# Query blocks of the mixing stage in another order: in pairs from the middle outwards, four heads of each in turn

## The chip, the cores and the metric

The kernel runs as one program on one core of a Trainium2 chip. The metric is the device time of one execution in microseconds (us). Before the change three runs gave 4028.39, 4029.53 and 4033.28 us, median 4029.53 us. Engines are named as in the profile: PE is TensorE, DVE is VectorE, ACT is ScalarE, POOL is GpSimd, SP is SyncE, whose queue here issues most loads.

## What is computed

One layer of a decoder trunk with two branches, for a prompt of 2048 positions and for 32 sample rows (8 requests of 4 positions). The change touches the stage that mixes positions of the prompt. Cut to what matters there:

```python
# branch A, mLSTM, over the chunks of the prompt, in order (a running state)
s   = einsum('bhtd,bhsd->bhts', qb, kb) * dmat
num = einsum('bhts,bhsv->bhtv', s, vb) + w_inter[..., None] * einsum('bhvd,bhtd->bhtv', C, qb)
h   = num / jnp.maximum(jnp.abs(den), jnp.exp(-m_t))[..., None]
C_new = w_prev[..., None, None] * C + einsum('bhs,bhsv,bhsd->bhvd', w_s, vb, kb)
h = h * lax.rsqrt(jnp.mean(h * h, axis=-1, keepdims=True) + EPS)

# branch B, attention of 8 heads on 2 groups of keys, for each block of 128 queries:
_, sel = lax.top_k(indexer_scores(iqb, iwb, ik, visible), topk)   # 256 keys for each query
s = einsum('btngd,btknd->btngk', q, k_sel) * (B_HD ** -0.5)
p = jax.nn.softmax(where(valid, s, -inf), axis=-1)
o = einsum('btngk,btknd->btngd', p, v_sel)
```

The kernel doesn't gather the chosen keys in the prompt: it scores a block against all keys up to its own and adds a stored mask of 0 or a large negative number. Block i (0 to 15) therefore has i + 1 tiles of 128 keys, and its work grows with i. Query blocks don't depend on each other; the chunks of branch A do.

## The kernel before, in words

The mixing stage (`prompt_mixing_phase`) runs from about 2208 to 3055 us of the span. All engines walk through one list of events, written by `mixing_events`, each taking from an event what concerns it, in order. The list goes over `heads`: n = 8 i + hd, block by block and head by head. One step n of the list holds, in this order:

- N of head n + 1 (DVE: reciprocal of the sum, L1962, and scaling of the probabilities, L1964);
- the first two T of head n (PE turns four tiles of 128 x 128 into one of two banks `pg`, L1690; ACT copies the bank to `probT`, L1820). A head has one T for four key tiles, so one or two for blocks 0 to 7, three or four for blocks 8 to 15;
- one event of branch A's next chunk, by hd: M1, M2 (twice), M3 (twice), M4 (twice), Y. These are PE matmuls (L1783, L1787, L1702) with DVE and ACT work between them: M1 needs on ACT `copy_k` (L1830) and the decay matrix (L1881) and on DVE the product `sd` (L2020), before its half of `slot` is free;
- at some n an event of the 32 sample rows (K, C, W, Z, V, U, from n = 12 to 114);
- the first S of head n + 3 (`scored[:1]`), then the T of head n that are left (`turned[2:]`), then the second S (`scored[1:]`). S is a piece of up to 1024 score columns: PE L1681, then DVE L1949, which adds the mask and takes the maximum. Blocks 0 to 7 have one piece, blocks 8 to 15 two;
- E of head n + 2 (ACT: exp, L1845);
- at hd 5 the event Q: ACT takes the row norms of branch A's chunk, four squares (L1907) and a square root (L1911) for which another function table is loaded;
- after heads 3 and 7 the event O: PE multiplies the turned probabilities of four heads with the values (L1720), ACT copies the result (L1855), POOL stores it (L1531).

Results of S, M1 to M4 and L pass through two halves of `slot` in turn; T and M1 through two banks of `pg` in turn. ACT and DVE do their part of the events strictly in the list's order: a copy for head n's third T stands behind whatever the list has for ACT before it. `prob` has three buffers, one for each head that is under way.

The SP queue loads queries and mask of a block (`load_a`) and the inputs of a chunk of branch A (`load_m`), two blocks ahead, and keys and values once (`load_resident`): `FIRST_KEYS` blocks of them first, the rest behind the loads of block 1.

Of the kernel before, what the change touches and what calls it, by code (L numbers as in the profile page):

```python
# [1351 lines left out]
FIRST_SAMPLE_STEP = 12  # L1352
FIRST_KEYS = 4

# [17 lines left out]
def mixing_events():  # L1372
# [5 lines left out]

    heads = [(i, hd) for i in range(NB) for hd in range(BH)]
    sample = sample_events()  # L1380
# [36 lines left out]
def prompt_mixing_phase(nc, c, d, first, load_first, inputs, load_inputs, load_memory, early):  # L1417
# [5 lines left out]
    with ExitStack() as ctx:  # L1423
# [104 lines left out]
        def store_oT(eng, i, kv):  # L1528

            n = 2 * i + kv  # L1530
            eng.dma_start(d["ybt"][4 * kv:4 * kv + 4, :, i * P:(i + 1) * P].rearrange("t p q -> p t q"),  # L1531
                          oT[n % 2][:, :, :]).then_inc(last_stored if n == 2 * NB - 1 else oT_stored[n % 2], 16)
# [4 lines left out]
        def _(sp):  # L1537
# [55 lines left out]
            sp.wait_ge(oT_ready, 2 * NB)  # L1593
            store_oT(sp, NB - 1, 1)

        @block.gpsimd
        def _(pool):
# [38 lines left out]
            for e in events:  # L1636
# [7 lines left out]
                elif e[0] == "Y":  # L1644
                    rows = slice(i * P, (i + 1) * P)
                    pool.wait_ge(ya_ready, 4 * (i + 1))
                    pool.dma_start(d["y"][rows, 0:D].rearrange("q (h e) -> q h e", h=AH), ya[:, :, :]).then_inc(ya_stored, 16)
                elif e[0] == "O" and 2 * i + e[2] + 1 < 2 * NB:
                    pool.wait_ge(oT_ready, 2 * i + e[2] + 1)
                    store_oT(pool, i, e[2])  # L1650
# [5 lines left out]
        def _(pe):  # L1656
# [15 lines left out]
            def score_piece(e):  # L1672
                _, i, hd, q = e
                p = i % 2
                if hd == 0 and q == 0:
                    pe.wait_ge(a_loaded[p], 32 * (i // 2 + 1))
                    pe.wait_ge(k_resident[i >= FIRST_KEYS], 16)
# [6 lines left out]
            def turn_group(e):  # L1684
                _, i, hd, q = e
                if q == 0:
                    pe.wait_ge(normed, BH * i + hd + 1)
                s = take_bank(e)
                for t in range(4 * q, min(4 * q + 4, i + 1)):
                    ins = turn(pg[:, s, (t % 4) * P:(t % 4 + 1) * P], prob[(BH * i + hd) % AHEAD][:, t * P:(t + 1) * P], c["ident"][:, :])  # L1690
                ins.then_inc(turned, 1)
# [12 lines left out]
            for e in events:  # L1704
# [5 lines left out]
                elif kind == "O":  # L1710
# [6 lines left out]
                    if 2 * i + kv:  # L1717
                        pe.wait_ge(oT_ready, 2 * i + kv)
                    for t in range(i + 1):
# [92 lines left out]
        def copy_group(act, e):  # L1812
# [3 lines left out]
            act.wait_ge(turned, n + 1)  # L1816
            if hd % 4 == 0 and 2 * i + hd // 4:
                act.wait_ge(o_mm, 2 * i + hd // 4)
            t0, t1 = 4 * q, min(4 * q + 4, i + 1)
# [14 lines left out]
        def _(act):  # L1834
# [3 lines left out]
            for e in events:  # L1838
                kind, i, p = e[0], e[1], e[1] % 2
                if kind == "E":  # L1840
                    hd = e[2]
                    act.wait_ge(nbias_ready, BH * i + hd + 1)
                    if i:
                        act.wait_ge(inverse, BH * (i - 1) + hd + 1)
                    nc.scalar.activation(prob[(BH * i + hd) % AHEAD][:, 0:(i + 1) * P], prob[(BH * i + hd) % AHEAD][:, 0:(i + 1) * P], ACT.Exp,  # L1845
                                         scale=SCALE, bias=mx[:, (BH * i + hd) % AHEAD, 1:2], accum_out=sums[:, hd:hd + 1]).then_inc(p_ready, 1)
                elif kind == "T":
                    copy_group(act, e)
                elif kind == "O":
                    kv = e[2]  # L1850
                    act.wait_ge(o_mm, 2 * i + kv + 1)
                    n = 2 * i + kv
                    if n >= 2:
# [60 lines left out]
        def _(dve):  # L1914
# [20 lines left out]
            for e in events:  # L1935
                kind, i, p = e[0], e[1], e[1] % 2
                if kind == "S":
                    hd = e[2]
                    q, b = e[3], (BH * i + hd) % AHEAD
                    lo, width = pieces((i + 1) * P)[q]  # L1940
                    s = slot_filled(dve, e)
                    if q:
                        after_slot(dve, ("S", i, hd, q - 1))
                    else:
                        dve.wait_ge(a_loaded[p], 32 * (i // 2 + 1))
                    if BH * i + hd >= AHEAD:
                        j, hp = divmod(BH * i + hd - AHEAD, BH)
                        dve.wait_ge(turned, bank_no[("T", j, hp, min(2 * q + 1, key_groups(j) - 1))] + 1)
                    nc.vector.tensor_tensor_reduce(out=prob[b][:, lo:lo + width], in0=slot[:, s, 0:width],  # L1949
                                                   in1=mk[p][:, lo:lo + width], scale=1.0,  # L1950
                                                   scalar=mx[:, b, 0:1] if q else TAKEN, op0=ALU.add, op1=ALU.max,
                                                   accum_out=mx[:, b, 0:1]).then_inc(slot_free[s], 1)
                    if q + 1 == key_pieces(i):
                        after_slot(dve, e)
                        if BH * i + hd >= AHEAD:
                            dve.wait_ge(p_ready, BH * i + hd - AHEAD + 1)
                        nc.vector.tensor_scalar(mx[:, b, 1:2], mx[:, b, 0:1], -SCALE, None, ALU.mult).then_inc(nbias_ready, 1)
                elif kind == "N":
                    n = BH * i + e[2]
                    b = n % AHEAD  # L1960
                    dve.wait_ge(p_ready, n + 1)
                    nc.vector.reciprocal(rsum[:, e[2]:e[2] + 1], sums[:, e[2]:e[2] + 1]).then_inc(inverse, 1)  # L1962
                    dve.wait_ge(inverse, n + 1)
                    nc.vector.tensor_scalar(prob[b][:, 0:(i + 1) * P], prob[b][:, 0:(i + 1) * P], rsum[:, e[2]:e[2] + 1], None,  # L1964
                                            ALU.mult).then_inc(normed, 1)
# [1905 lines left out]
```

## Time and profile before

| | us |
|---|---|
| median of 3 runs (lowest, highest) | 4029.53 (4028.39, 4033.28) |
| the profiled execution's own time | 4027.08 |
| its span | 4025.5 |
| PE busy in the span | 3879.9 (96%) |
| DVE busy | 2919.6 (73%) |
| ACT busy | 1414.2 (35%) |
| POOL busy | 1661.6 (41%) |
| first and last PE start in the mixing stage | 2222.12, 3053.3 |

The profiled execution took 4027.08 us, and its span is 4025.5 us: 1.6 us lie outside the span. Its mean granted TensorE clock is 0.985 of full speed. A busy share is an average over stages that have different limits; the mixing stage is a fifth of the span, from slice 23 to slice 31 of the page's 40.

### The profile page before, as it was taken

Reading aid. Unit: us, or ns where it says so; the run is one execution under the profiler, and the core shown is the slowest. Engines: PE = TensorE matmul, PEld = TensorE weight load, DVE = VectorE, ACT = ScalarE, POOL = GpSimd, SP = SyncE. Lnnn points to the kernel's source line nnn. Section 1 sums busy time; section 2 is a strip of 40 time slices with the busy share of each in tenths; the row PEclk is TensorE's granted clock in tenths of the full one; section 3 lists DMA queues with packets and bytes.
Section 4 is the critical chain, followed back from the end, with each engine's and each line's share of the span. In section 5 each row is a group of like instructions: output and inputs, shape, how many; then the busy total and the mean of one; then the engine's idle time right before and its main releaser. Section 6 shows DMA issues by size and latency. Waiting matters only on the chain. (4 is left out here: it accounts for less than half of the span.)

```text
span 4025.5 us, 41935 instructions
## 1 busy us (share of the span) xinstructions
PE 3879.9 (96%) x14574; PEld 2324.4 (58%) x14574; DVE 2919.6 (73%) x3887; ACT 1414.2 (35%) x2616; POOL 1661.6 (41%) x1513
## 2 busy tenths in 40 slices
PE   8899999999999999999999699999998899999999
PEld 4555555564456566666665466555553788854444
DVE  4589989779999999999996566555454577653333
ACT  4411211156234423433431566555553322111111
POOL 0000035449687556666664232122103666552111
PEclk9999999999999999999999899999999999999999
DMA  5312222330111121121211643222132755531111
GB/s 220 91 53 67 65 82 85 117 121 36 60 60 64 53 71 64 63 70 63 69 61 60 186 119 105 66 90 78 61 101 79 228 166 169 173 127 68 39 53 46
DMA packets 290825, 367.35 MB, mean 91 GB/s; under 512 B 72223, under 2 KB 219443, under 8 KB 287926
## 3 DMA queue, kind: packets, MB, share of 16 engines
q1 hardware_dynamic: 250890, 249.79, 20.3%
q0 software_dynamic: 18608, 85.26, 5.7%
q10 hardware_dynamic: 21120, 29.66, 2.4%
q8 instruction: 115, 1.88, 0.2%
q14 instruction: 92, 0.75, 0.1%
HBM read 235.11 MB, written 128.23 MB: 90 GB/s over the span
## 5 line engine op out<-in xcount | busy, mean ns | idle before, releaser
L1306 DVE MAX8 best<-score 128x8 f32<-128x384 f32 (+13 forms) x448 | 639.7, 1428 | 26.5 <-POOL score L1274 11.6
L1308 DVE MATCH_REPLACE8 score<-best,score 128x384 f32<-128x384 f32 (+13 forms) x448 | 631.2, 1409 | 0.0
L1063 PE MATMUL pr<-xnT,w_row 128*128 128x347 f32 (+1 forms) x960 | 298.5, 458 | 0.0
L389 PE MATMUL pg<-xnT,wt 128*128 128x416 f32 x800 | 282.4, 516 | 0.0
L1215 POOL TENSOR_TENSOR kT<-kT 128x347 f32<-128x347 f32 (+1 forms) x240 | 193.7, 807 | 212.0 <-ACT kT L1133 204.8
L1681 PE MATMUL mix_slot<-mix_kT,mix_bq 128*128 128x512 f32 (+3 forms) x640 | 271.0, 539 | 10.3 <-DVE mix_mx L1949 4.3
L1720 PE MATMUL mix_po<-mix_probT,mix_v 128*128 128x512 f32 x544 | 240.8, 596 | 5.2 <-ACT mix_probT L1820 4.3
L1063 PEld LDWEIGHTS pr<-xnT,w_row 128*128 128x128 f32 x960 | 180.7, 190 | 106.5 <-issue 10.4
L1133 ACT COPY kT<-pr 128x347 f32<-128x347 f32 (+1 forms) x240 | 106.5, 445 | 351.9 <-PE pr L1063 341.8
L389 PEld LDWEIGHTS pg<-xnT,wt 128*128 128x128 f32 x800 | 153.1, 192 | 127.7 <-issue 127.6
L1215 POOL TENSOR_TENSOR kT<-kT,sm 128x347 f32<-128x347 f32 (+1 forms) x179 | 159.8, 893 | 125.4 <-ACT sm L1133 122.8
L1063 PE MATMUL pr<-t_room,w_row 128*128 128x347 f32 (+1 forms) x640 | 203.1, 460 | 0.0
L1093 ACT ACTIVATE relu<-relu,iws 128x512 f32<-128x512 f32 (+3 forms) x304 | 186.7, 661 | 5.0
L1820 ACT COPY mix_probT<-mix_pg 128x512 f32<-128x512 f32 (+3 forms) x320 | 153.8, 524 | 86.1 <-PE mix_pg L1690 85.6
L1133 ACT COPY sm<-pr 128x347 f32<-128x347 f32 (+1 forms) x180 | 80.2, 445 | 287.3 <-PE pr L1063 237.8
L1720 PEld LDWEIGHTS mix_po<-mix_probT,mix_v 128*128 128x128 f32 x544 | 102.1, 191 | 129.9 <-issue 128.7
L1531 POOL DMA_DIRECT2D ybt_scr<-mix_oT x31 | 24.4, 787 | 369.2 <-ACT mix_oT L1855 349.2
L1088 ACT ACTIVATE relu<-pi 128x1024 f32<-128x1024 f32 (+3 forms) x152 | 139.7, 919 | 98.4 <-POOL score L1270 47.4
L1063 PEld LDWEIGHTS pr<-t_room,w_row 128*128 128x128 f32 x640 | 121.9, 192 | 70.1 <-issue 7.0
L1681 PEld LDWEIGHTS mix_slot<-mix_kT,mix_bq 128*128 128x128 f32 x640 | 111.2, 192 | 88.5 <-issue 70.8
L995 PE MATMUL pi<-ikT,iq 64*128 64x512 f32 (+3 forms) x608 | 139.9, 577 | 12.6 <-ACT relu L1088 8.8
L1063 PE MATMUL pr<-t_room,w0b 128*128 128x347 f32 (+1 forms) x480 | 150.4, 455 | 0.0
(637 smaller groups left out, 8086.4 us busy)
## 6 DMA issues: line engine op xcount, KB each, us to landing
gt_scr<-kT SPq DMA_DIRECT2D x40, 694.0 KB, 3.3
out_gm<-gt_scr ACTq DMA_DIRECT2D x32, 520.0 KB
gt_scr<-kT SPq DMA_DIRECT2D x20, 692.0 KB, 4.2
wt<-in_w_in SPq DMA_DIRECT2D x22, 512.0 KB, 4.0
w0a<-in_w_in SPq DMA_DIRECT2D x11, 1024.0 KB, 6.7
w_row<-in_w_in SPq DMA_DIRECT2D x10, 1024.0 KB, 6.7
qt_scr<-kT POOLq DMA_DIRECT2D x8, 1040.0 KB, 4.2
early<-ybt_scr SPq DMA_DIRECT2D x4, 2080.0 KB, 10.7
```

What stands on the lines that cost most here:

```text
L389: ins = nc.tensor.matmul(pg[0:m, g, 0:GW], w[:, k, 0:m], c["xnT"][:, k, g * GW:(g + 1) * GW], start=k == 0, stop=k == KT - 1)
L995: ins = nc.tensor.matmul(pi[:, piece % 2, e, 0:width], iq[t % 2][half, h2, :], c["ikT"][half, lo:lo + width], start=True, stop=True)
L1063: ins = nc.tensor.matmul(pr[:, b, 0:w], lhs, rhs, start=k == 0, stop=k == 3)
L1088: nc.scalar.activation(relu[piece % 2][:, :, 0:width], pi[:, piece % 2, :, 0:width], ACT.Relu, scale=float(ID) ** -0.5).then_inc(relu_step, 1)
L1093: nc.scalar.activation(rl, rl, ACT.Copy, scale=iws[:, blocks[t], 2 * h2 + e:2 * h2 + e + 1]).then_inc(relu_ready, 1)
L1133: nc.scalar.copy(dst, pr[:, b, 0:GATE_WIDTHS[n % GATE_PASSES]]).then_inc(row_out, 1)
L1215: nc.gpsimd.tensor_tensor(o[:, slot, :], o[:, slot, :], term, ALU.add).then_inc(added, 1)
L1306: nc.vector.max(best[:, :], sc).then_inc(top_step, 1)
L1308: nc.vector.match_replace(sc, best[:, :], sc, TAKEN).then_inc(top_step, 1)
L1681: ins = mm(slot[:, s, a:a + m], bq[p][:, hd, :], kT[:, hd // 4, lo + a:lo + a + m], start=True, stop=True)
L1720: ins = mm(po[:, :], v[:, t, kv * HD:(kv + 1) * HD], probT[:, t, :, :], start=t == 0, stop=t == i)
L1820: nc.scalar.copy(probT[:, t0:t1, hd % 4, :], pg[:, n % 2, 0:(t1 - t0) * P].rearrange("p (t q) -> p t q", q=P)).then_inc(bank_free[n % 2], 1)
```

## The change

The list of heads no longer goes through blocks 0 to 15. Blocks are taken in pairs from the middle outwards, (7, 8), (6, 9), (5, 10), ... (0, 15), and within a pair four heads of the smaller block, four of the larger, the other four of the smaller, the other four of the larger. A group of four heads is still one O. Branch A's chunks keep their order, one chunk for eight steps of the list, now by the place n in the list instead of by block and head. All counts that engines wait for go by the place in the list (`HEAD_AT`, `GROUP_AT`, `BLOCK_AT`). `FIRST_KEYS` becomes 8, since the first block of the list is block 7. No instruction of the mathematics is added or removed.

```diff
-FIRST_KEYS = 4
+FIRST_KEYS = 8
+BLOCK_ORDER = [b for n in range(NB // 2) for b in (NB // 2 - 1 - n, NB // 2 + n)]
+GROUP_ORDER = [(b, kv) for n in range(NB // 2) for kv in range(KV) for b in BLOCK_ORDER[2 * n:2 * n + 2]]
+HEAD_ORDER = [(b, BH // KV * kv + x) for b, kv in GROUP_ORDER for x in range(BH // KV)]
+BLOCK_AT = {b: n for n, b in enumerate(BLOCK_ORDER)}
+GROUP_AT = {g: n for n, g in enumerate(GROUP_ORDER)}
+HEAD_AT = {h: n for n, h in enumerate(HEAD_ORDER)}
...
-    heads = [(i, hd) for i in range(NB) for hd in range(BH)]
+    heads = HEAD_ORDER
...
-        if i + 1 < NB:
-            m, *x = memory[hd]
-            events.append((m, i + 1, *x))
-        elif hd in (1, 2):
-            events.append(("L", hd - 1))
+        step, at = n // BH + 1, n % BH
+        if step < NB:
+            m, *x = memory[at]
+            events.append((m, step, *x))
+        elif at in (1, 2):
+            events.append(("L", at - 1))
...
-        if hd == 5 and i + 1 < NB:
-            events.append(("Q", i + 1))
+        if at == 5 and step < NB:
+            events.append(("Q", step))
...
-            def load_a(i):
-                p, rows = i % 2, slice(i * P, (i + 1) * P)
-                if i >= 2:
-                    after_slot(sp, ("S", i - 2, BH - 1, key_pieces(i - 2) - 1))
+            def load_a(n):
+                i, p = BLOCK_ORDER[n], n % 2
+                rows = slice(i * P, (i + 1) * P)
+                if n >= 2:
+                    earlier = BLOCK_ORDER[n - 2]
+                    after_slot(sp, ("S", earlier, BH - 1, key_pieces(earlier) - 1))
```

Three places show what moves. In these rows `mix_slot<-mix_kT,mix_bq` is an S, `mix_pg<-ident,...` a T (one matmul for a tile), `mix_slot<-sm_C` and the like branch A, `mix_pb<-out_w` a sample event, `mix_po` an O.

First PE, in the second half of block 13: before the change, from the last T of head 5 to the O of the block's heads 4 to 7:

```order
L1690 MATMUL mix_pg<-ident,early 128x128 x6
L1681 MATMUL mix_slot<-mix_kT,mix_bq 128x512
L1681 MATMUL mix_slot<-mix_kT,mix_bq 128x384
L1690 MATMUL mix_pg<-ident,mix_prob 128x128 x8
L1702 MATMUL mix_slot<-sm_C 128x257 x2
L1771 MATMUL mix_pb<-out_w 32x128 x4
L1681 MATMUL mix_slot<-mix_kT,mix_bq 128x512 x2
L1690 MATMUL mix_pg<-ident,mix_prob 128x128 x6
L1681 MATMUL mix_slot<-mix_kT,mix_bq 128x512
L1681 MATMUL mix_slot<-mix_kT,mix_bq 128x384
```

The same place after the change, from an S that stands just before the last T of the same head to the same O and the next group's first T:

```order
L1693 MATMUL mix_slot<-mix_kT,mix_bq 128x256
L1702 MATMUL mix_pg<-ident,early 128x128 x14
L1714 MATMUL mix_slot<-sm_C 128x257 x2
L1783 MATMUL mix_pb<-out_w 32x128 x4
L1693 MATMUL mix_slot<-mix_kT,mix_bq 128x256
L1702 MATMUL mix_pg<-ident,early 128x128 x6
L1702 MATMUL mix_pg<-ident,mix_prob 128x128 x8
L1783 MATMUL mix_pb<-out_w 32x128 x4
L1693 MATMUL mix_slot<-mix_kT,mix_bq 128x256
L1702 MATMUL mix_pg<-ident,mix_prob 128x128 x6
L1732 MATMUL mix_po<-mix_probT,mix_v 128x512 x14
L1702 MATMUL mix_pg<-ident,early 128x128 x2
```

Between the T of one large head and those of the next stood pieces of 1024 and 896 columns; now there stands one piece of 256 columns, of the small block that follows, and none between the last T and the O.

Second ACT, at the same place. Before:

```order
L1820 COPY mix_probT<-mix_pg 128x4x128 x3
L1820 COPY mix_probT<-mix_pg 128x2x128
L1845 ACTIVATE early,mix_sums<-early,mix_mx 128x1792
L1907 ACTIVATE sm_C,mix_den<-sm_C,mix_den 128x256 x4
L1911 ACT_TABLE_LOAD
L1911 ACTIVATE mix_den<-mix_den,eps 128x4
L1820 COPY mix_probT<-mix_pg 128x4x128 x3
L1820 COPY mix_probT<-mix_pg 128x2x128
L1845 ACT_TABLE_LOAD
L1845 ACTIVATE early,mix_sums<-early,mix_mx 128x1920
```

After the change:

```order
L1832 COPY mix_probT<-mix_pg 128x4x128 x3
L1832 COPY mix_probT<-mix_pg 128x2x128
L1858 ACTIVATE mix_prob,mix_sums<-mix_prob,mix_mx 128x1792
L1920 ACTIVATE sm_C,mix_den<-sm_C,mix_den 128x256 x4
L1924 ACT_TABLE_LOAD
L1924 ACTIVATE mix_den<-mix_den,eps 128x4
L1832 COPY mix_probT<-mix_pg 128x4x128 x3
L1832 COPY mix_probT<-mix_pg 128x2x128
L1858 ACT_TABLE_LOAD
L1858 ACTIVATE early,mix_sums<-early,mix_mx 128x256
```

ACT's own order is the same but for the size of the exp that follows.

Third PE, from M1 to the first M2 of the chunk that starts just after this O. Before:

```order
L1783 MATMUL mix_slot<-sm_C 128x128 x4
L1787 MATMUL mix_pg<-ident,sm_C 128x128 x4
L1771 MATMUL mix_pb<-out_w 32x128 x4
L1681 MATMUL mix_slot<-mix_kT,mix_bq 128x512 x2
L1690 MATMUL mix_pg<-ident,early 128x128 x7
L1681 MATMUL mix_slot<-mix_kT,mix_bq 128x512
L1681 MATMUL mix_slot<-mix_kT,mix_bq 128x384
L1690 MATMUL mix_pg<-ident,mix_prob 128x128 x8
L1702 MATMUL mix_slot<-mix_cT,sm_C 128x257 x2
```

After the change:

```order
L1795 MATMUL mix_slot<-sm_C 128x128 x4
L1799 MATMUL mix_pg<-ident,sm_C 128x128 x4
L1783 MATMUL mix_pb<-out_w 32x128 x4
L1693 MATMUL mix_slot<-mix_kT,mix_bq 128x256
L1702 MATMUL mix_pg<-ident,early 128x128 x2
L1714 MATMUL mix_slot<-mix_cT,sm_C 128x257 x2
```

M1 always falls on the first head of a small block's group now, so that only that block's S and T stand before M2.

## Rows read from the trace of the kernel before

**Rows 1.** The page: busy us and share of the span, instructions.

```profile
PE 3879.9 (96%) x14574; PEld 2324.4 (58%) x14574; DVE 2919.6 (73%) x3887; ACT 1414.2 (35%) x2616; POOL 1661.6 (41%) x1513
```

**Rows 2.** Windows: stretch, its length, busy of each engine, clock, DMA share, GB/s.

```profile
2208.00:2222.00 14.00, 0.00 (x0) 0.00 (x0) 0.00 (x0) 0.00 (x0) 2.64 (x8) 0.58 0.71 167
2222.00:2241.20 19.20, 11.44 (x42) 8.38 (x42) 8.17 (x28) 9.75 (x27) 10.75 (x15) 0.77 0.87 254
2241.20:2267.02 25.82, 17.51 (x66) 12.47 (x67) 12.50 (x57) 14.37 (x49) 0.79 (x1) 0.83 0.62 181
2267.02:2293.40 26.38, 21.04 (x94) 14.74 (x93) 16.49 (x61) 17.53 (x52) 8.51 (x9) 0.98 0.74 197
2293.40:2474.59 181.19, 173.32 (x776) 116.21 (x775) 115.47 (x327) 120.39 (x289) 56.88 (x61) 1.00 0.42 118
2474.59:2639.30 164.71, 157.07 (x658) 96.76 (x657) 91.44 (x234) 95.05 (x201) 30.08 (x32) 1.00 0.26 81
2639.30:2988.24 348.94, 340.95 (x1536) 190.86 (x1535) 175.31 (x390) 186.57 (x352) 74.74 (x78) 1.00 0.27 81
2988.24:3054.60 66.36, 61.55 (x241) 33.77 (x239) 21.54 (x37) 31.24 (x50) 1.50 (x2) 1.00 0.13 36
```

**Rows 3.** Waits of PE from 2241.2 to 2988.24: total us, times, longest.

```profile
PE mix_slot L1702 <- DVE mix_sd L2020: 11.7, 8, 2.8
PE mix_pg L1690 <- ACT mix_probT L1820: 8.4, 10, 1.5
```

**Rows 4.** Timeline of PE in block 13, heads 5 and 6: start, us, idle before.

```profile
2885.07 0.82 PE L1690 MATMUL mix_pg<-ident,early 128*128 128x128 f32 x6
2885.73 1.67 PE L1681 MATMUL mix_slot<-mix_kT,mix_bq 128*128 128x512 f32 x4
2887.23 1.04 PE L1690 MATMUL mix_pg<-ident,mix_prob 128*128 128x128 f32 x8
2888.11 1.03 PE L1702 MATMUL mix_slot<-sm_C 128*128 128x257 f32 x4
2889.43 1.98 PE L1681 MATMUL mix_slot<-mix_kT,mix_bq 128*128 128x512 f32 x4
2892.44 0.82 PE L1690 MATMUL mix_pg<-ident,mix_prob 128*128 128x128 f32 x5 [1.03 <-ACT mix_probT L1820]
```

**Rows 5.** Timeline of ACT at the same place.

```profile
2886.45 1.80 ACT L1845 ACTIVATE early<-early,mix_mx 128x1792 f32<-128x1792 f32 x1
...
2888.24 0.50 ACT L1907 ACTIVATE sm_C<-sm_C,mix_den 128x256 f32<-128x256 f32 x1
...
2890.32 1.28 ACT L1911 ACT_TABLE_LOAD   x1
2891.62 0.30 ACT L1911 ACTIVATE mix_den<-mix_den,eps 128x4 f32<-128x4 f32 x1
2891.82 1.05 ACT L1820 COPY mix_probT<-mix_pg 128x512 f32<-128x512 f32 x2
...
2894.01 1.28 ACT L1845 ACT_TABLE_LOAD   x1
```

**Rows 6.** Timeline of PE, head 6 of blocks 8, 10 and 14.

```profile
2566.93 0.33 PE L1690 MATMUL mix_pg<-ident,early 128*128 128x128 f32 x1 [1.08 <-ACT mix_probT L1820]
...
2686.06 0.55 PE L1690 MATMUL mix_pg<-ident,mix_prob 128*128 128x128 f32 x3 [0.61 <-ACT mix_probT L1820]
...
2966.98 0.44 PE L1690 MATMUL mix_pg<-ident,early 128*128 128x128 f32 x2 [1.47 <-ACT mix_probT L1820]
```

**Rows 7.** Timeline of PE, first M2 after M1, in blocks 1 and 7.

```profile
2272.47 0.89 PE L1702 MATMUL mix_slot<-mix_cT,sm_C 128*128 128x257 f32 x3 [2.60 <-DVE mix_sd L2020]
...
2480.02 0.67 PE L1702 MATMUL mix_slot<-mix_cT,sm_C 128*128 128x257 f32 x2 [0.23 <-DVE mix_sd L2020]
```

**Rows 8.** Timeline of PE, last O of the stage (block 15).

```profile
3039.96 1.53 PE L1720 MATMUL mix_po<-mix_probT,mix_v 128*128 128x512 f32 x3 [0.91 <-ACT mix_probT L1820]
```

**Rows 9.** Windows around an early wait of PE and just behind another.

```profile
2235.10:2239.50 4.40, 0.09 (x1) 0.00 (x0) 2.61 (x9) 2.86 (x3) 1.26 (x1) 0.78 1.07 343
...
2247.60:2251.00 3.40, 2.94 (x8) 2.20 (x9) 1.17 (x10) 1.37 (x5) 0.00 (x0) 0.53 0.79 196
```

More of the change, by code:

```diff
@@ L1593, in _ @@
             sp.wait_ge(oT_ready, 2 * NB)
-            store_oT(sp, NB - 1, 1)
+            store_oT(sp, *GROUP_ORDER[-1])
         @block.gpsimd
@@ L1647, in _ @@
                     pool.dma_start(d["y"][rows, 0:D].rearrange("q (h e) -> q h e", h=AH), ya[:, :, :]).then_inc(ya_stored, 16)
-                elif e[0] == "O" and 2 * i + e[2] + 1 < 2 * NB:
-                    pool.wait_ge(oT_ready, 2 * i + e[2] + 1)
+                elif e[0] == "O" and GROUP_AT[i, e[2]] + 1 < len(GROUP_ORDER):
+                    pool.wait_ge(oT_ready, GROUP_AT[i, e[2]] + 1)
                     store_oT(pool, i, e[2])
@@ L1673, in score_piece @@
                 _, i, hd, q = e
-                p = i % 2
+                n = BLOCK_AT[i]
+                p = n % 2
                 if hd == 0 and q == 0:
-                    pe.wait_ge(a_loaded[p], 32 * (i // 2 + 1))
+                    pe.wait_ge(a_loaded[p], 32 * (n // 2 + 1))
                     pe.wait_ge(k_resident[i >= FIRST_KEYS], 16)
@@ L1716, in _ @@
                             pe.wait_ge(bank_free[x], (last + 2 - x) // 2)
-                    if 2 * i + kv:
-                        pe.wait_ge(oT_ready, 2 * i + kv)
+                    if GROUP_AT[i, kv]:
+                        pe.wait_ge(oT_ready, GROUP_AT[i, kv])
                     for t in range(i + 1):
@@ L1816, in copy_group @@
             act.wait_ge(turned, n + 1)
-            if hd % 4 == 0 and 2 * i + hd // 4:
-                act.wait_ge(o_mm, 2 * i + hd // 4)
+            if hd % 4 == 0 and GROUP_AT[i, hd // 4]:
+                act.wait_ge(o_mm, GROUP_AT[i, hd // 4])
             t0, t1 = 4 * q, min(4 * q + 4, i + 1)
@@ L1840, in _ @@
                 if kind == "E":
[L1841 to L1846, printed above, removed]
+                    n = HEAD_AT[i, e[2]]
+                    act.wait_ge(nbias_ready, n + 1)
+                    if n >= BH:
+                        act.wait_ge(inverse, n - BH + 1)
+                    scores = prob[n % AHEAD][:, 0:(i + 1) * P]
+                    nc.scalar.activation(scores, scores, ACT.Exp, scale=SCALE, bias=mx[:, n % AHEAD, 1:2],
+                                         accum_out=sums[:, n % BH:n % BH + 1]).then_inc(p_ready, 1)
                 elif kind == "T":
@@ L1850, in _ @@
                     kv = e[2]
-                    act.wait_ge(o_mm, 2 * i + kv + 1)
-                    n = 2 * i + kv
+                    n = GROUP_AT[i, kv]
+                    act.wait_ge(o_mm, n + 1)
                     if n >= 2:
@@ L1937, in _ @@
                 if kind == "S":
-                    hd = e[2]
-                    q, b = e[3], (BH * i + hd) % AHEAD
+                    n, q, at = HEAD_AT[i, e[2]], e[3], BLOCK_AT[i]
+                    b = n % AHEAD
                     lo, width = pieces((i + 1) * P)[q]
@@ L1942, in _ @@
                     if q:
-                        after_slot(dve, ("S", i, hd, q - 1))
+                        after_slot(dve, (*e[:3], q - 1))
                     else:
-                        dve.wait_ge(a_loaded[p], 32 * (i // 2 + 1))
-                    if BH * i + hd >= AHEAD:
-                        j, hp = divmod(BH * i + hd - AHEAD, BH)
+                        dve.wait_ge(a_loaded[at % 2], 32 * (at // 2 + 1))
+                    if n >= AHEAD:
+                        j, hp = HEAD_ORDER[n - AHEAD]
                         dve.wait_ge(turned, bank_no[("T", j, hp, min(2 * q + 1, key_groups(j) - 1))] + 1)
                     nc.vector.tensor_tensor_reduce(out=prob[b][:, lo:lo + width], in0=slot[:, s, 0:width],
-                                                   in1=mk[p][:, lo:lo + width], scale=1.0,
+                                                   in1=mk[at % 2][:, lo:lo + width], scale=1.0,
                                                    scalar=mx[:, b, 0:1] if q else TAKEN, op0=ALU.add, op1=ALU.max,
@@ L1954, in _ @@
                         after_slot(dve, e)
-                        if BH * i + hd >= AHEAD:
-                            dve.wait_ge(p_ready, BH * i + hd - AHEAD + 1)
+                        if n >= AHEAD:
+                            dve.wait_ge(p_ready, n - AHEAD + 1)
                         nc.vector.tensor_scalar(mx[:, b, 1:2], mx[:, b, 0:1], -SCALE, None, ALU.mult).then_inc(nbias_ready, 1)
                 elif kind == "N":
-                    n = BH * i + e[2]
-                    b = n % AHEAD
+                    n = HEAD_AT[i, e[2]]
+                    b, at = n % AHEAD, slice(n % BH, n % BH + 1)
                     dve.wait_ge(p_ready, n + 1)
-                    nc.vector.reciprocal(rsum[:, e[2]:e[2] + 1], sums[:, e[2]:e[2] + 1]).then_inc(inverse, 1)
+                    nc.vector.reciprocal(rsum[:, at], sums[:, at]).then_inc(inverse, 1)
                     dve.wait_ge(inverse, n + 1)
-                    nc.vector.tensor_scalar(prob[b][:, 0:(i + 1) * P], prob[b][:, 0:(i + 1) * P], rsum[:, e[2]:e[2] + 1], None,
+                    nc.vector.tensor_scalar(prob[b][:, 0:(i + 1) * P], prob[b][:, 0:(i + 1) * P], rsum[:, at], None,
                                             ALU.mult).then_inc(normed, 1)
```

6 lines of the change are left out of this document (3 added, 3 removed).

## The prediction, made before the changed kernel was run

> **What bounds the kernel now.** I began with the page's busy shares [rows 1]: PE is busy in 96% of the span, so what PE waits for, and nothing else, is what the order of blocks can change. Then I cut the mixing stage into stretches at its O events [rows 2]. The reader is to see three regions. Up to 2267 us PE is far from full: 14 us without a matmul while the first loads come, then 42 us with 29 us of busy PE at a clock of 0.77 to 0.83. From 2267 to 2988 PE is busy but for 5.3, 7.9, 7.6 and 8.0 us. The last stretch, block 15, has 4.8 us idle, since no scores are left to do between the last turns. ACT and DVE are each busy for little more than half of it. The waits [rows 3] name two causes above all: M2 waits for `sd` (11.7 us, once for each chunk while blocks are small) and a T waits for ACT's copy of an earlier T (8.4 us). So before the change small blocks suffer from branch A's chain and large ones a little from ACT. The last thing I read is how that second wait comes about, as it decides this case.
>
> **What the move takes away.** Nothing of the mathematics goes, so the sum is one of waits. Each wait costs its idle time and about 0.17 us more, because a matmul record is that much longer than the distance to the next one (four of the second S: 1.67 us, next start after 1.50 [rows 4]). At most all of the following goes: 2241 to 2267, 8.3 us idle, 3.0 of slow clock (17% of 17.5 busy), some 12 restarts, together 13; 2267 to 2293, 5.3 and restarts, 6; 2293 to 2475, 7.9 and restarts, 9; 2475 to 2639, 7.6 and about 15 restarts, 10; 2639 to 2988, 8.0 and restarts, 9 [rows 2]. Sum 47 us. The last stretch ends as before: four heads of block 15 with nothing behind them. At the start, the 19 us before 2241 are branch A's first chunk, during which PE now has three S of 8 tiles where it had three of 1 tile. A tile of S costs 0.214 us (seven tiles in 1.50 us), a T tile 0.11 (eight in 0.88) [rows 4]. 21 tiles more are 4.5 us of work moved under that chain; the first T then starts some 2 us later, since exp and scaling are longer. Gain 2. I take 49 us gained and, in the next parts, all waits of the new order as cost.
>
> **ACT behind the norms, the main term.** Take block 13. After the last T of head 5 ACT copies, does an exp of 1.80 us from 2886.45, four squares from 2888.24, a table load of 1.28, a square root, and only at 2891.82 the copy that PE's third T of head 6 needs [rows 5]. Meanwhile PE does seven tiles of S from 2885.73, two T, half of M4, a sample event, and eight tiles of S from 2889.43 [rows 4]: 15 tiles of S, 3.2 us, cover ACT, and 1.03 us stays uncovered. In the new order the event Q falls on the second head of the larger block's group, always (list place 8 k + 5). The S that stands between these T is then one piece of the small block that follows: 2 tiles instead of 15 in the second half of block 13. ACT's row of work is unchanged. So the wait becomes 1.03 + 13 x 0.214 = 3.8 us. This is a subtraction, not a model: only cover is removed. The same for each larger block, with its own wait of before (1.08, 0.68, 0.61, 0.99, 0.85, 1.03, 1.47 for blocks 8 to 14; three of them in [rows 6]) and its own difference of tiles (2, 4, 6, ... 14 in the first group of a pair, 16 for block 15, one more in the second): 1.5, 1.5, 1.9, 2.7, 3.0, 3.6, and 4.1 for block 14, where a sample event that block lacked before covers 0.4, twice each with 0.2 more in the second, and 4.9 once for block 15: 43 us idle. With 15 restarts of 0.25 (third T, bank and copy have to follow each other) 47 us. Low end: if PE comes late to the place for other reasons the wait of each is halved, 23; high end 60, if the copy of K, a sample event of ACT, comes in between in blocks 8 to 12.
>
> A rule of the Trainium skill bears on this. The row shows the table load as 1.28 us, with 0.02 us before the square root starts [rows 5]. "ScalarE: Activation LUTs", section "What ACT_TABLE_LOAD costs", puts a drain of about 1.38 us on top of the load, 2.66 us in all. By that rule each of the 15 waits would be 1.4 us longer, some 21 us more in the sum; by the row there is no such drain between the squares, the load and the root. The trace decides, and I take the row.
>
> **ACT behind the next exp.** One head later the second table load (1.28 us [rows 5]) and a short exp stand before the copies of head 7 of the group. PE has a T, a sample event and the small S to do: about 1.2 us idle for blocks 13 to 15, 0 to 0.5 for the others, where the small S is still 4 to 8 tiles. Sum 7 us (0 to 12).
>
> **O no longer covered.** Between the last T of a group and its O stood the second S. Now the O follows at once and waits for two copies. The last O of the stage already does so and waits 0.91 us [rows 8]. For 15 more groups of large blocks, 0.6 to 1.0 us each by the tiles of the last T, 12 us (8 to 16).
>
> **M2 behind M1.** M1 to M2 takes ACT and DVE the same time in all small blocks, so the idle time depends on the block's S and T in between: 2.60 us with 2 tiles, 0.23 with 8 [rows 7], 2.83 with 1. The seven values for 2 to 8 tiles sum to 8.8. M1 now always falls on the first head of a small group, which each small block has twice: 2 x 8.8 + 2.8 for block 0 once, with restarts 23 us (20 to 26). The 11.7 us of before [rows 3] are within the 49 taken away, so this term alone has doubled.
>
> **Slots.** In the third and fourth head of a small group PE puts pieces of a large block into both halves of `slot` and DVE adds masks, scales a head of up to 16 tiles and does M3 between them; 0.2 to 0.5 us each for the first two and the last three pairs, 5 us (0 to 10).
>
> **The clock.** After two of the early waits the rows show slow stretches: in 2235.1 to 2239.5 PE stood almost still and the clock reads 0.78, that is partly the lower level, 1.2 GHz; behind a wait of 2.83 us the stretch 2247.6 to 2251.0 reads 0.53 [rows 9]. Some ten of the new waits are 2.7 us or longer. If each brings about 3.4 us of half clock, half of which PE hides in waits for copies, it is 0.9 us each: 9 us (0 to 24).
>
> **Loads.** `load_a` of a large block waits for the last S of the one before and is used five heads later, more than 17 us; at the start block 7's mask and eight blocks of keys (0.75 MB more than before at 254 GB/s [rows 2], 3 us) are due only after branch A's first chunk, which ends 12 us after the first matmul. I cost them at nothing; what covers them is that chunk, and without it they would cost 3 us.
>
> **Sum.** 47 + 7 + 12 + 23 + 5 + 9 = 103 us of new waits, less 49: 54 us, of which I take 50, as the waits of one head partly stand for each other. The profiled execution took 4027.1 us (1.6 us around its span of 4025.5) and the median of the runs is 2.4 us above it: 4029.5 + 50 = 4080 us.
>
> **The rivals.**
> First, faster: ACT isn't late. The place is Q in the larger block's group, the price 47 + 7 + 12 us and with them the clock's 9. Then only M2 and slots remain, 28 us against 49 gained: 4029.5 - 21 = 4008 us. It decides from the point at which the O of 8 to 14 us, in which ACT idles, lets ACT run ahead of the list. For it: ACT is busy for 55% only, and the large blocks' waits of before are 1 us. Against it: ACT can't run ahead of T events that PE has not yet done, and the list is in order; the cover removed is counted in rows.
> Second, slower still: the clock falls after nearly every wait. "TensorE: Matmul & The Clock Gate", section "Why this matters for your kernels", says that one long idle gap between bursts of matmuls puts TensorE back to its lower clock. By the rows as a mechanism of this kernel: 15 waits with 3.4 us each at half clock, none hidden, and the 7 in pairs with a second one, are about 25 us instead of 9: 4096 us. For it: the early stretches [rows 9]. Against it: the stretch from 2267 has waits of 2.6 us and a clock of 0.98 [rows 2, 7].
> Third, slower by loads: if queries, masks or the second half of the keys come late at each of 8 pairs by 2 to 3 us: 4100 us. Against it is a DMA share of 0.27 to 0.42 after 2293 [rows 2].
> Fourth, no change: early gains and new waits cancel, at half of the ACT terms: 4029.5 + 50 - 47 = about 4032 us.
>
> **How the numbers follow.** Chances: my forecast 0.66, the clock 0.14, the loads 0.05, no more than half the ACT terms 0.04, faster 0.11. The low ends of the terms give 4029.5 + 23 + 0 + 8 + 20 + 0 + 0 - 49 = 4032 us, the high ends 4029.5 + 60 + 12 + 16 + 26 + 10 + 24 - 49 = 4128 us. All terms at one end together is unlikely; I leave out the outer part of both and take 4042 to 4110 us, which holds all but 2 in 10 with the faster case left out. A measurement of this kernel can tell 0.2%, 8 us, from no change. Faster 0.11, within 0.2% 0.03, slower 0.86.
>
> **What would show it.** In the profile after: the wait of `mix_pg` for the copy into `mix_probT` rises from 8.4 us to 40 or more, with single waits of 3 to 5 us in the last pairs, each behind a table load on ACT; `mix_po` waits for `mix_probT` about 16 times; `mix_slot` for `mix_sd` 20 us in 16 waits; the stretch up to block 7's first O is shorter in idle time than before; and some stretches after 2300 show a granted clock under 1. The last pairs, not the first, are where PE's idle share is highest. I am wrong if the waits for `mix_probT` stay near 10 us, or if the stage's PE idle time falls.

## The result, and the profile after

The changed kernel takes 4112.48 us (median of 5 runs, 4109.61 to 4115.77) against 4029.53 us: 83 us slower, ratio 1.0204, interval 1.0193 to 1.0216. The forecast was slower, 4080 us, range 4042 to 4110. Direction and mechanism came out as argued; the size did not, and the time lies 2.5 us outside the range.

The windows over the whole stage, of after (columns as in [rows 2]):

```profile
2219.00:3140.30 921.30, 825.35 (x3403) 497.32 (x3403) 429.70 (x1130) 477.84 (x1018) 185.49 (x198) 0.95 0.29 87
```

and of before:

```profile
2222.00:3054.00 832.00, 782.88 (x3403) 473.20 (x3403) 440.91 (x1130) 474.34 (x1018) 183.25 (x198) 0.99 0.33 96
```

The same 3403 matmuls take 42 us more of busy time at a clock of 0.95 instead of 0.99, and PE's idle time grows by 47 us. Behind the stage nothing changes: 971 us in both.

Between first and last matmul start the stage grew from 831.2 to 920.5 us, by 89 us. The time grew by 83: in these two traces the stage begins 2.9 us earlier after the change and what stands behind it is 0.9 us shorter, and the profiled execution of before lies 2.5 us under its median. Such differences come between all versions here: the first matmul of the stage starts at 2219.0 to 2222.1 us, and what stands behind the stage takes 967 to 973 us.

The waits of PE in the stage, of after (total us, times, longest):

```profile
PE mix_pg L1702 <- ACT mix_probT L1832: 51.9, 38, 4.3
PE mix_slot L1714 <- DVE mix_sd L2033: 17.1, 13, 2.4
...
PE mix_po L1732 <- ACT mix_probT L1832: 10.2, 13, 0.9
```

and of before, over the whole stage too ([rows 3] have a part of it):

```profile
PE mix_slot L1702 <- DVE mix_sd L2020: 13.2, 9, 2.8
PE mix_pg L1690 <- ACT mix_probT L1820: 11.2, 14, 1.7
```

The copy of turned tiles went from 11.2 to 51.9 us, `sd` from 13.2 to 17.1, and the O events, which waited for copies 4.3 us in all, now wait 10.2.

The timeline of PE in the first group of block 13, of after, to be laid beside [rows 4]:

```profile
2827.31 1.03 PE L1714 MATMUL mix_slot<-sm_C 128*128 128x257 f32 x4
2828.28 0.43 PE L1783 MATMUL mix_pb<-out_w 128*32 128x128 f32 x8
2828.63 0.91 PE L1693 MATMUL mix_slot<-mix_kT,mix_bq 128*128 128x384 f32 x2
2832.41 1.54 PE L1702 MATMUL mix_pg<-ident,mix_prob 128*128 128x128 f32 x6 [2.87 <-ACT mix_probT L1832]
2834.30 1.94 PE L1702 MATMUL mix_pg<-ident,early 128*128 128x128 f32 x8 [0.34 <-ACT mix_probT L1832]
2836.17 0.66 PE L1783 MATMUL mix_pb<-out_w 128*32 128x128 f32 x8
...
2840.37 5.82 PE L1732 MATMUL mix_po<-mix_probT,mix_v 128*128 128x512 f32 x13 [0.93 <-ACT mix_probT L1832]
```

and of ACT there:

```profile
2826.43 1.80 ACT L1858 ACTIVATE early<-early,mix_mx 128x1792 f32<-128x1792 f32 x1
...
2830.30 1.28 ACT L1924 ACT_TABLE_LOAD   x1
2831.59 0.30 ACT L1924 ACTIVATE mix_den<-mix_den,eps 128x4 f32<-128x4 f32 x1
2831.79 1.05 ACT L1832 COPY mix_probT<-mix_pg 128x512 f32<-128x512 f32 x2
...
2834.44 1.28 ACT L1858 ACT_TABLE_LOAD   x1
```

ACT's row from its exp to the copy takes 5.36 us, as before (5.37 [rows 5]); only PE's cover shrank. The block's second group, the place of [rows 4] itself, shows it best:

```profile
2884.91 0.82 PE L1702 MATMUL mix_pg<-ident,early 128*128 128x128 f32 x6
2886.27 1.06 PE L1702 MATMUL mix_pg<-ident,early 128*128 128x128 f32 x8 [0.55 <-ACT mix_probT L1832]
...
2892.28 0.93 PE L1702 MATMUL mix_pg<-ident,early 128*128 128x128 f32 x6 [3.08 <-ACT mix_probT L1832]
```

From the last T of head 5 to the third T of head 6 it takes 7.37 us, before (2885.07 to 2892.44 [rows 4]) and after. With 13 tiles of S fewer in it PE waits 0.55 + 3.08 us instead of 1.03.

Then, in the first group, look at what comes behind the wait: eight T matmuls take 1.94 us where they took 1.04 [rows 4], a sample event 0.66 instead of 0.43. That is half clock. The windows there, and after the second such wait of the stage:

```profile
2832.30:2839.10 6.80, 6.35 (x29) 4.55 (x30) 2.52 (x11) 4.35 (x9) 0.24 (x1) 0.50 0.00 0
2839.10:2852.60 13.50, 12.57 (x33) 5.61 (x32) 0.81 (x5) 1.46 (x4) 2.27 (x3) 1.00 0.17 59
...
2333.90:2337.30 3.40, 3.40 (x13) 3.04 (x14) 0.45 (x2) 3.37 (x7) 0.00 (x0) 0.50 0.58 74
```

Before the change there was no such stretch between 2268 us and the stage's end. Now there are 18 from 2283 us on, 88.7 us together. Of the 15 waits behind Q all but one (2.46 us, at 2553.0) have such a stretch, which starts within 2 us of their end. The other four stretches come behind M2's waits of 1.73, 2.06, 2.05 and 2.37 us in branch A's last four chunks (from 2857.6 us on); those of 1.53, 1.53 and 2.29 us in the three chunks before have none.

To part the two causes I took all matmuls of the stage from first start to last: "work" is the sum of the usual distances between starts by shape, "slow" what a matmul takes longer within a half-clock stretch (at most its own length again), "wait" the rest.

| run | median us | stage | work | slow | wait |
|---|---|---|---|---|---|
| before | 4029.5 | 831.2 | 735.8 | 6.8 | 88.6 |
| after | 4112.5 | 920.5 | 736.6 | 41.8 | 142.0 |
| large_first | 4031.0 | 835.4 | 735.7 | 8.1 | 91.7 |
| q_under_o | 4078.2 | 886.4 | 736.6 | 28.4 | 121.3 |
| q_preload | 4043.1 | 849.4 | 736.5 | 14.6 | 98.3 |
| m1_later | 4089.0 | 895.3 | 737.1 | 28.5 | 129.8 |
| both_moved | 4029.3 | 834.1 | 736.4 | 7.3 | 90.4 |
| whole_blocks | 4045.6 | 854.2 | 736.7 | 20.0 | 97.5 |
| filled | 4093.7 | 900.5 | 774.1 | 13.0 | 113.4 |
| fill_elsewhere | 4156.7 | 959.4 | 776.0 | 39.7 | 143.6 |
| no_root | 4071.3 | 879.4 | 736.6 | 18.7 | 124.2 |
| after_s | 4035.1 | 840.3 | 735.6 | 5.4 | 99.4 |
| before_q | 4020.9 | 830.2 | 736.3 | 18.9 | 75.0 |
| before_s | 4004.0 | 810.0 | 735.6 | 12.2 | 62.2 |

The change: wait +53.4, slow +35.0, work +0.8 us. The division between slow and wait is mine and good to a few us where both meet.

### The profile page after: what moved, and what is told of

It reads as the page before. It is cut to its first block and busy times, and to the rows that moved or that the text cites. A ratio compares the mean times of both kernels' runs of the same rounds, so it can differ in the third digit from the quotient of the medians.

```text
span 4110.9 us, 41934 instructions
## 1 busy us (share of the span) xinstructions
PE 3919.9 (95%) x14574; PEld 2344.9 (57%) x14574; DVE 2907.1 (71%) x3887; ACT 1417.7 (34%) x2616; POOL 1663.7 (40%) x1513
## 5 line engine op out<-in xcount | busy, mean ns | idle before, releaser
L1306 DVE MAX8 best<-score 128x8 f32<-128x384 f32 (+13 forms) x448 | 639.6, 1428 | 26.3 <-POOL score L1274 11.3
L1732 PE MATMUL mix_po<-mix_probT,mix_v 128*128 128x512 f32 x544 | 243.9, 602 | 11.8 <-ACT mix_probT L1832 10.2
L2033 DVE TENSOR_TENSOR mix_sd<-mix_slot,mix_dmat 128x512 f32<-128x512 f32 x16 | 11.1, 692 | 209.2 <-ACT mix_dmat L1894 175.8
```

What stands on the lines that cost most here:

```text
L1306: nc.vector.max(best[:, :], sc).then_inc(top_step, 1)
L1732: ins = mm(po[:, :], v[:, t, kv * HD:(kv + 1) * HD], probT[:, t, :, :], start=t == 0, stop=t == i)
```

## The experiments

The kernel before ran beside each: 4027.55 us in the first set of four, 4029.77 in the second, 4029.67 in the third.

**large_first.** The larger block first in each pair, all else as changed:

```diff
-FIRST_KEYS = 8
+FIRST_KEYS = 9
-BLOCK_ORDER = [b for n in range(NB // 2) for b in (NB // 2 - 1 - n, NB // 2 + n)]
+BLOCK_ORDER = [b for n in range(NB // 2) for b in (NB // 2 + n, NB // 2 - 1 - n)]
```

> The changed kernel with the larger block first in each pair ((8, 7), (9, 6), ...), and 9 blocks of keys loaded first. Branch A's events then meet the other block's heads: M1 falls on the large group's first head, Q on the small group's second head, which has no third T. Theory (the waits come from where branch A's events meet the large heads, and the slow clock follows from the waits): PE's waits for mix_probT fall from 51.9 to about 15 us, for mix_sd from 17.1 to under 4, the half-clock stretches after 2280 us nearly go, time 4010 to 4040 us. Rival (any interleaving with small blocks leaves the large heads' turns uncovered, wherever Q is): waits stay over 35 us and the time over 4080 us.

Measured 4030.96 us, ratio to before 1.0007 (0.9998 to 1.0017). Its waits:

```profile
PE mix_pg L1702 <- ACT mix_probT L1832: 11.6, 20, 1.1
PE mix_po L1732 <- ACT mix_probT L1832: 10.3, 13, 0.9
PE mix_slot L1693 <- DVE mix_mx L1962: 6.9, 6, 3.5
...
PE mix_slot L1693 <- DVE mix_sd L2033: 3.7, 4, 1.3
```

Beside before, 3 of the 83 us are left, which is within the noise, with the blocks interleaved as much as in the changed kernel, and no half-clock stretch comes after 2280 us. So it is not interleaving that costs, but which heads branch A's Q and M1 meet.

**q_under_o.** Q to the large group's fourth head, ahead of the O:

```diff
+        if at == 0 and n:
+            events.append(("Y", step - 1))
-        if step < NB:
+        if step < NB and at < 7:
...
-        if at == 5 and step < NB:
+        if at == 7 and step < NB:
             events.append(("Q", step))
```

> The changed kernel with Q (squares, table load, root) moved from the second to the fourth head of the large group, just before the O event, so that ACT does it while PE does the O of 8 to 14 us; Y one step later. Theory: the 15 waits behind Q (40.4 us idle) go, the second table load no longer stands before a copy, waits for mix_probT fall to 10 to 15 us, and with them most of the half-clock stretches (about 34 us lost now); mix_sd's 17 us stay. Time 4035 to 4055 us. Rival (the slow clock belongs to the pattern of turns and small pieces, not to the waits): only the waits go, 4065 to 4080 us.

Measured 4078.24 us, ratio 1.0124 (1.0101 to 1.0147): outside the theory's range and inside the rival's, so this run alone doesn't rule the rival out. But it isn't as the rival has it either, since the half-clock stretches after 2280 us went from 18 to 11, ten of them behind waits of M2. The waits for copies went as expected, but another rose:

```profile
PE mix_slot L1716 <- DVE mix_sd L2035: 34.9, 13, 3.8
...
PE mix_pg L1704 <- ACT mix_probT L1834: 12.2, 23, 1.7
```

**q_preload.** The same, and the exp table loaded at once behind the root:

```diff
                     nc.scalar.activation(den[:, 1, :], den[:, 3, :], ACT.Sqrt, ...
+                    nc.scalar.activation(junk[:, 0:1], c["eps"][:, 0:1], ACT.Exp)
```

> The run with Q under the O (4078 us), plus the tiny exp behind Q's root. There the waits for mix_sd had risen from 17.1 to 34.9 us. Theory (the exp table was then loaded by the decay matrix's exp, 1.28 us within the chain from M1 to M2): mix_sd falls back to 17 to 20 us, time 4050 to 4062 us. Rival (it is DVE's Y, now at the same head, that delays sd): mix_sd stays over 30 us and the time within 5 us of 4078.

Measured 4043.08 us, ratio 1.0038 (1.0026 to 1.0050), 7 us under the theory's range; `sd` fell from 34.9 to 18.7 us, as the theory had it. The second table load had moved from behind Q into the chain from M1 to M2. One instruction on a [128, 1] operand gave 35 us: 23 of wait, 14 of slow clock.

**m1_later.** Only M1 moved, Q where the change has it:

```diff
+        if at == 0 and n:
+            events.append(("Y", step - 1))
-        if step < NB:
-            m, *x = memory[at]
+        if step < NB and at > 0:
+            m, *x = memory[at - 1]
```

> The changed kernel with branch A's M events one head later (M1 on the second head of the small group, so that two large score pieces stand between M1 and M2; Y on the next chunk's first head); Q stays on the large group's second head. Theory: PE's waits for mix_sd fall from 17.1 us to under 2 and nothing else changes: 4090 to 4098 us, or some us less where the wait also cost clock. Rival (the 17 us only move to another wait): within 4 us of 4112.

Measured 4088.95 us, ratio 1.0147 (1.0126 to 1.0168), 23.5 us less than the changed kernel and just under the range, as the theory allowed: 12 of wait and 13 of slow clock. `sd` before M2 fell from 17.1 to 1.6 us, but part of it moved, as the rival had it: S pieces now wait 8.9 us for `sd`, 10 times. So 12 us less of waiting brought twice its own length.

**filled** and **fill_elsewhere.** Useless matmuls, repeated scores into the same room; in the first in PE's wait behind Q, in the second, as a control, where PE doesn't wait (`filled` holds how often such a piece is computed, `extra` how many 512-column pieces are added):

```diff
-                for a, m in pieces(width, 512):
-                    ins = mm(slot[:, s, a:a + m], ...
+                for _ in range(filled.get(e, 1)):
+                    for a, m in pieces(width, 512):
+                        ins = mm(slot[:, s, a:a + m], ...
```

```diff
-                for a, m in pieces(width, 512):
+                for a, m in [(0, 512)] * extra.get(e, 0) + pieces(width, 512):
```

> The changed kernel with useless work: the small score piece that stands before the third T behind Q is computed again, 2 to 19 times into the same room, so that PE is busy for 1.6 to 3.7 us of the 2.0 to 4.3 us in which it waited. The waits' length is ACT's and stays. Theory (the clock falls because PE waits there): half-clock stretches go, time 4112 less 20 to 34 us, 4078 to 4092 us, though the kernel does 35 us more matmul work. Rival (the clock has another cause, or costs little): 4110 to 4125 us.

> Control for the run with the waits filled by useless score pieces (4094 us): about as much useless work (some 38 us of 512-column score matmuls), but ahead of the large score piece on the small group's third head, where PE doesn't wait. Theory: it comes on top, 4112 plus 36 to 40 us, the slow clock as in the changed kernel. Rival (more matmul work anywhere keeps the clock up): under 4135 us.

Measured 4093.68 us (ratio 1.0161, 1.0144 to 1.0178) and 4156.71 us (1.0317, 1.0301 to 1.0332), 2 and 5 us above the theory's ranges and far from the rivals'. The stage's windows, filled:

```profile
2219.00:3120.00 901.00, 836.81 (x3569) 502.52 (x3569) 429.52 (x1130) 477.22 (x1017) 185.33 (x198) 0.98 0.31 89
```

and the control:

```profile
2219.00:3180.50 961.50, 864.02 (x3495) 513.97 (x3495) 430.00 (x1130) 478.11 (x1017) 185.89 (x198) 0.95 0.29 84
```

38 us of useless work in the waits made the kernel 19 us faster and brought the clock from 0.95 to 0.98; 39 us of it elsewhere made it 44 us slower with the clock at 0.95. In the filled kernel no half-clock stretch is left behind Q:

```profile
2282.00:2849.00 567.00, 532.19 (x2231) 324.56 (x2230) 281.37 (x746) 312.50 (x671) 117.72 (x123) 1.00 0.28 76
```

The three that remain, 13.7 us, stand behind M2's waits of 1.74, 2.06 and 2.05 us, which weren't filled. This shows that the slow clock behind Q comes from PE standing still there and not from the order of turns and scores. Of the 29 us of slow clock that went, 19 arrived in the time; some 9 us of the useless work didn't fit in the waits.

**no_root.** A square in Q instead of the square root, so no table load there or behind (branch A's norm is not computed as in the reference):

```diff
-                    nc.scalar.activation(den[:, 1, :], den[:, 3, :], ACT.Sqrt, ...
+                    nc.scalar.activation(den[:, 1, :], den[:, 3, :], ACT.Square, ...
```

> The changed kernel with a square in place of Q's square root, so that no table is loaded in Q nor for the next exp; branch A's norm is not the reference's. Each of the 15 waits behind Q is 1.28 us shorter, so 40 us become about 21, and the exp after it 1.28 us shorter. Theory (the slow clock comes from these waits, and a wait of 1 to 2 us brings it less often): slow-clock loss from 42 to about 20 to 25 us, time 4060 to 4072 us. Rival (the slow clock belongs to the pattern of turns, not to the waits): the loss stays near 40 us, 4085 to 4092 us.

Measured 4071.32 us, ratio 1.0102 (1.0087 to 1.0118): wait -18, slow -23. Waits only 1.28 us shorter took more than half of the slow clock away: 7 stretches are left after 2280 us, four behind M2's waits and three behind waits of 2.01, 2.23 and 2.99 us for copies. The time is in the theory's range, the slow clock 1 us under it.

**whole_blocks.** The same order of blocks, eight heads of each:

```diff
-GROUP_ORDER = [(b, kv) for n in range(NB // 2) for kv in range(KV) for b in BLOCK_ORDER[2 * n:2 * n + 2]]
+GROUP_ORDER = [(b, kv) for b in BLOCK_ORDER for kv in range(KV)]
```

> The changed kernel with the same order of blocks, but all eight heads of a block together. Theory: a small block's Q finds no third T, so the waits behind Q come once for each large block instead of twice (about 20 us), M1's wait once for each small block (9 to 11 us), half of the slow clock: 4050 to 4070 us. Rival (it is the order of blocks, not the groups of four, that costs): 4100 to 4115 us. Rival (groups of four cost all of it): 4025 to 4035 us.

Measured 4045.58 us, ratio 1.0043 (1.0027 to 1.0058), 4 us under the range that the theory gave. The wait for copies was 25.0 us in 18 waits and `sd` 11.3, about as said; `mix_po` waited for copies 4.2 us against 10.2 in the changed kernel.

**both_moved.** The changed kernel with M1 one head later, Q ahead of the O and the tiny exp (the edits above together).

> The changed kernel's order of blocks, with branch A's events one head later (M1 on the second head of the small group), Q on the large group's fourth head before the O, and a tiny exp behind Q's root, so that the exp table is loaded while PE does the O. Theory (waits behind Q 40 us, behind M1 17 us, and some 35 us of slow clock that follow from them are what the change costs, against waits gained): waits for mix_probT 10 to 15 us, for mix_sd under 10, hardly a half-clock stretch after 2280 us; time 4005 to 4025 us, under the kernel before. Rival (interleaving has a cost of its own, as the run with the larger block first, 4031 us, may say): 4030 to 4045 us.

Measured 4029.27 us, ratio 1.0003 (0.9994 to 1.0012), between the two ranges. The change's whole cost is gone, and no half-clock stretch comes after 2280 us, but the theory's gain over before didn't come. Waits are 90.4 us against 88.6: 11.6 us for copies, 9.9 us at O and some at slots stand where the small blocks' waits stood.

**after_s and before_s.** Branch A three heads later: M1 on the fourth head and Q on the eighth, each ahead of an O, M4 and Y in the next eight; with the tiny exp. In the kernel before (the changed kernel has `step` and `at` for `i + 1` and `hd`):

```diff
-        if i + 1 < NB:
-            m, *x = memory[hd]
-            events.append((m, i + 1, *x))
-        elif hd in (1, 2):
-            events.append(("L", hd - 1))
+        late = hd < 3
+        if n >= 3 and i + 1 - late < NB:
+            m, *x = memory[(hd - 3) % BH]
+            events.append((m, i + 1 - late, *x))
+        elif i + 1 == NB and hd in (3, 4):
+            events.append(("L", hd - 3))
...
-        if hd == 5 and i + 1 < NB:
+        if hd == 7 and i + 1 < NB:
```

> The changed kernel's order of blocks with the same shift of branch A: M1 on the small group's fourth head, M2 and M3 on the large group's heads, Q and the tiny exp on its fourth head ahead of its O, M4 and Y on the next small group's heads. Theory: as with both moved (4029 us), some waits of slots less: 4020 to 4030 us, hardly a half-clock stretch after 2280 us. Rival (M events among the large heads' turns add waits for ACT): 4032 to 4045 us.

> The kernel before, in its own order of blocks, with branch A three heads later: M1 on head 3, just ahead of an O, M2 and M3 on heads 4 to 7, Q and the tiny exp on head 7 ahead of the other O, M4 and Y on heads 0 to 2 of the next block. Theory (M1's chain of 4.8 us and Q's of 5 us cost nothing while PE has an O to do): waits for mix_sd 12.7 to under 5 us, time 4008 to 4016 us, beside 4021 for Q alone moved. Rival (in small blocks O is too short): 4017 to 4024 us.

after_s: 4035.07 us, ratio 1.0014 (1.0005 to 1.0023), in the rival's range but not by its mechanism: the waits of turns for ACT's copies are 11.3 us, no more than with both moved. What came instead are waits for a half of `slot`: S pieces wait for `sd` 12.6 us in 15 waits, and M1 waits for DVE's masks (`mix_mx`) 10.2 us in 14. before_s: 4003.95 us, ratio 0.9939 (0.9926 to 0.9953), 26 us faster than before and better than I expected. Its waits:

```profile
PE mix_pg L1692 <- DVE early L1967: 4.9, 3, 3.6
PE mix_slot L1683 <- DVE mix_mx L1952: 3.9, 2, 3.4
PE mix_slot L1704 <- DVE mix_sd L2023: 3.0, 2, 1.6
PE mix_pg L1692 <- ACT mix_probT L1822: 2.3, 2, 1.7
```

Both waits of [rows 3] are nearly gone. It is the fastest version measured, with the blocks in their old order.

**before_q.** The kernel before with only Q ahead of the second O, Y one head later and the tiny exp.

> The kernel before, in its own order of blocks, with Q moved to head 7 before the O, Y one step later and the tiny exp behind Q. Theory: of the 11.2 us of waits for mix_probT the 7 behind Q in blocks 8 to 14 go, 8 to 10 us with what follows; 4018 to 4022 us beside 4027.5. Rival (small blocks, where O is too short to hide 5 us of Q and table loads, lose as much): 4025 to 4032 us.

Measured 4020.89 us, ratio 0.9979 (0.9970 to 0.9988), in the theory's range, but the trace bears its reason out only in part. The waits behind Q in blocks 8 to 14 are gone. In the small blocks, as the rival had it, copies now come late behind the two table loads: PE waits 3.68, 1.94, 0.79 and 1.32 us at 2269.7, 2298.1, 2331.1 and 2364.9. In all the waits fell by 13.6 us, while the slow clock rose by 12.1, and the stage is only 1.0 us shorter. The profiled execution is 8.5 us shorter, and 7.5 of that lie outside the stage, where the change did nothing. That the number met the forecast is in part luck, and where the gain comes from stays open.

## Why the prediction was wrong

Right, by its own steps:
- ACT behind the norms: 43 us idle forecast, 40.4 us measured in 15 waits, from 1.8 to 4.3 us and growing with the pairs. In blocks 11 to 15 a part of the wait stands already at the same head's first T: nine waits of 0.24 to 0.66 us, 4.1 in all. Together they are 44.5 us, for block 13 3.42 and 3.63 against 3.6 and 3.8 forecast. The subtraction of cover held within 0.6 us each; it gave up to 0.6 too little at the small end and up to 0.4 too much at the large end, so that the sum is closer than its parts. large_first, q_under_o, q_preload and no_root show the cause.
- ACT behind the next exp: 7 us forecast beyond the last block's 2.8; about half came, nine waits of 3.8 us in all behind Q's.
- O no longer covered: 12 us forecast, 10.2 measured. M2 behind M1: 20.5 us idle forecast; 17.1 in 13 waits named `sd` (one of them, 1.6 us, is the first chunk's and was there before), and three of 4.7 us in all put down to issue. Slots: 5 forecast, 5.7 named `mix_mx`.
- All waits less those gained: 94 less 46 is 48 us forecast, 53 measured. Only this difference is measured; what was gained isn't, by itself. The loads cost nothing, as forecast.

The table load stood at 1.28 us, and the root started 0.01 us behind it. So the trace went on disagreeing with the rule of the Trainium skill ("ScalarE: Activation LUTs", section "What ACT_TABLE_LOAD costs") that the prediction had weighed, of a drain on top of the load.

Wrong: the clock, a term with the right mechanism and much too small. The step said that "some ten of the new waits are 2.7 us or longer", that each brings 3.4 us of half clock, "half of which PE hides in waits for copies", 9 us in all (0 to 24). With the 3 us of early slow clock that I had among the gains this made 6 us net; it was 35, above even the term's high end. Three things were off. The length of 2.7 us was no condition: there are 18 slow stretches, of which only 7 come behind a wait as long as that, 7 behind shorter waits behind Q, down to 1.82 us, and 4 behind M2, which the step didn't count at all. They are longer, 88.7 us together instead of 34. And PE hides little of them: the stage has 82 us more of half clock than before, which could cost 41, and 35 of those arrived. Within the 18 stretches PE stood idle for only 7.6 us, so there was hardly a wait in which slow work could hide. Had the clock term been 38 instead of 9 us, the forecast would have been 4109 us. The rows that should have warned me were there: a wait of 2.83 us was followed by 3.4 us at 0.53 [rows 9]. I set against them a wait of 2.6 us without one, and took a length as the condition.

The rival by the clock gate had the mechanism and 4096 us, also short, and by a slip in its sum: 15 stretches of 3.4 us at half clock cost 25 us, so "the 7 in pairs with a second one", if that means 7 stretches more, are left out. With them it would be 37 us and some 4108 us, near the 35 us measured. But the stretches came otherwise than it says: one of the 15 had none, M2's waits brought four, and four behind Q were 6.8 to 13.7 us long. The page of the Trainium skill that it leant on, "TensorE: Matmul & The Clock Gate", section "Why this matters for your kernels", warns of one long idle gap between bursts of matmuls. The runs differ from it in that waits behind Q of 1.82 to 2.25 us, 52 to 56 us apart, were each followed by half clock, while the next one, of 2.46 us, was not, nor were waits of 1.84 and 2.60 us in the small blocks of the kernel before. The faster rival fell: ACT didn't run ahead. The loads' rival and the one of no change fell too.

What stays open is why the same wait brings half clock at one place and not at another. filled and its control tie it to PE's standing still there, and in the filled kernel M2's wait of 2.37 us has no stretch where the changed kernel's has one; they don't say what else within the surrounding microseconds counts. Also open is where the early gain went in both_moved: its listed waits name places, but no run took them away one by one.

## What to carry to other kernels

When two streams of work share one ordered list, reordering one of them moves every event of the other to new neighbours; for each engine, list what stands behind the slow events (here a table switch and four squares) and how much of the bound engine's work covers them, before and after. Put such an event just ahead of the bound engine's longest piece that needs nothing from it, if that piece is long enough (in before_q's small blocks it wasn't), and load the table that is needed next at once. And price a regular wait of PE at more than its length: here 53 us of waits cost 35 us more in clock.

## What the runs showed of the hardware that I had not expected

- Useless matmuls in PE's waits made the kernel faster, 4112.5 to 4093.7 us, by the clock (half-clock time in the stage 101 to 33 us).
- A wait of 1.82 us was followed by 3.4 us at half clock in the changed kernel; waits of 1.84 and 2.60 us in the kernel before, at 2298 and 2272 us, were not. The length of one wait doesn't tell.
- The copy between two functions' table loads ran without a load of its own (2831.79 us, between 2830.30 and 2834.44), so here the exp table was needed back only at the next exp, wherever that fell.
